# A hybrid encoder layer with 32 experts: from the eleventh unit on, the down projection goes ahead of the next up projection

## The reference, cut to what matters

```python
def hier_moe(x, w_group, b_group, w_router, b_router, w_e1, w_e3, w_e2):
    ...
    for gi in range(N_GROUPS):
        h = jax.nn.silu(jnp.einsum('md,edf->mef', xt, w_e1[gi])) * jnp.einsum('md,edf->mef', xt, w_e3[gi])
        out = out + jnp.einsum('mef,efd->md', h * combine[:, gi, :, None], w_e2[gi])
    return out.reshape(n, t, d)
```

## Time and profile before

| what | value |
|---|---|
| median of 3 runs | 898.16 us |
| the three runs | 896.39, 898.16, 898.18 us |
| the profiled execution's own time | 896.4 us |
| its span in the profile | 894.6 us |
| PE busy | 765.0 us, 86% |
| DVE, ACT, POOL busy | 363.6, 228.2, 156.5 us |
| DMA, mean over the span | 196 GB/s |
| HBM read | 164.43 MB |

### The profile page before, as it was taken

The page is one execution under the profiler, slowest core; times in us unless marked ns, Lnnn a source line. Parts: engine busy times, 40 slices in busy tenths (PEclk is TensorE's granted clock), DMA queues, the critical chain, the costliest instruction groups (busy, mean ns, idle before and its releaser), DMA issues.

```text
span 894.6 us, 11943 instructions
## 1 busy us (share of the span) xinstructions
PE 765.0 (86%) x4700; PEld 554.5 (62%) x4700; DVE 363.6 (41%) x632; ACT 228.2 (26%) x444; POOL 156.5 (17%) x157
## 2 busy tenths in 40 slices
PE   6999999999799999999999999953999996476600
PEld 6999985774466999999999954531333332122100
DVE  4899927997676310110111022465111111010168
ACT  5214231736576522222222100110111111010100
POOL 4000001000313243335333300012011111000100
PEclk9999999999898999999999999975999999688955
DMA  8323225021100732222222078484999999999872
GB/s 327 139 75 97 77 71 188 13 66 38 47 1 13 277 113 83 84 74 83 81 83 95 13 287 370 153 348 165 390 418 417 419 421 420 420 420 421 307 262 82
DMA packets 38467, 175.73 MB, mean 196 GB/s; under 512 B 7064, under 2 KB 7624, under 8 KB 25992
## 3 DMA queue, kind: packets, MB, share of 16 engines
q1 hardware_dynamic: 33496, 163.66, 47.7%
q0 software_dynamic: 4912, 11.28, 3.4%
HBM read 164.43 MB, written 16.78 MB: 203 GB/s over the span
## 4 chain that ended last, share of the span: by engine, by line
PE 73%; DMA 9%; DVE 8%; SPq 7%; issue 2%; ACT 1%; POOLq 0%; ACTq 0%
PE PS L673 38%; PE PS L975 7%; PE PS L865 7%; DMA expert<-in_w_e 7%; PE PS L656 5%; SPq L495 4%; PE PS L997 3%; PE PS L783 2%; SPq L498 2%; PE PS L749 2%; PE PS L763 2%; PE PS L731 2%; DVE x_tiles L1699 1%; PE PS L826 1%; PE PS L929 1%
## 5 line engine op out<-in xcount | busy, mean ns | idle before, releaser
L673 PE MATMUL PS<-x_hi,w_hi 128*128 128x288 f32 (+2 forms) x656 | 142.5, 299 | 9.4 <-DVE x_lo L1310 8.5
L673 PE MATMUL PS<-x_lo,w_hi 128*128 128x288 f32 (+2 forms) x656 | 141.9, 298 | 0.0
L673 PE MATMUL PS<-x_hi,w_lo 128*128 128x288 f32 (+2 forms) x656 | 141.6, 298 | 0.0
L975 PE MATMUL PS<-expert,moe_tmp 128*64 128x512 f32 (+2 forms) x576 | 112.5, 630 | 31.3 <-DMA expert<-in_w_e 30.0
L673 PEld LDWEIGHTS PS<-x_hi,w_hi 128*128 128x128 f32 x656 | 106.7, 191 | 9.7 <-POOL w_lo L455 8.5
L1060 ACT ACTIVATE w_hi<-raw_ring 128x1024 fp32r<-128x1024 f32 (+1 forms) x57 | 57.1, 1002 | 214.4 <-PE PS L673 209.9
L673 PEld LDWEIGHTS PS<-x_lo,w_hi 128*128 128x128 f32 x656 | 106.6, 191 | 0.0
L673 PEld LDWEIGHTS PS<-x_hi,w_lo 128*128 128x128 f32 x656 | 106.5, 191 | 0.0
L975 PEld LDWEIGHTS PS<-expert,moe_tmp 128*64 128x64 f32 (+2 forms) x576 | 36.1, 134 | 97.4 <-issue 95.5
L455 POOL TENSOR_TENSOR w_lo<-raw_ring,w_hi 128x1024 fp32r<-128x1024 f32 (+1 forms) x33 | 70.2, 2127 | 136.3 <-ACT w_hi L1060 136.3
L1327 DVE SCALAR_TENSOR_TENSOR conv_z<-attn_tmp,wdw,conv_z 128x576 f32<-128x576 f32 x120 | 90.6, 813 | 0.3
(11 more groups left out here) (286 smaller groups left out, 1021.1 us busy)
## 6 DMA issues: line engine op xcount, KB each, us to landing
expert<-in_w_e SPq DMA_DIRECT2D x96, 1024.0 KB, 26.2
raw_ring<-in_w_gate_t SPq DMA_DIRECT2D x24, 512.0 KB, 3.3
raw_ring<-in_w_glu_t SPq DMA_DIRECT2D x8, 512.0 KB, 4.8
raw_ring<-in_w_como_t SPq DMA_DIRECT2D x8, 512.0 KB, 3.5
heads<-in_w_out SPq DMA_DIRECT2D x1, 4096.0 KB, 14.0
x_rows<-x_tiles SPq DMA_DIRECT2D x8, 512.0 KB, 5.1
expert_out<-expert_rows SPq DMA_DIRECT2D x8, 512.0 KB, 6.5
x_raw<-in_xT SPq DMA_DIRECT2D x4, 576.0 KB, 6.0
```

The source lines that it names most:

```text
L673: mm = pe.matmul(half(name, s, 128, cols[s]), w[:, n % 2, at + 128 * k:at + 128 * k + 128], x[:, k, t0[s]:t0[s] + cols[s]], start=(k == 0 ...
L975: mm = pe.matmul(PS[r0:r0 + nr, 2, :].rearrange("p (s f) -> p s f", s=2), xgT[:, k, r0:r0 + nr], w13[s % NB][:, :, k, :], start=(k == 0), ...
```

## The change

A constant `UNPIPED = 10` is added. For u below 10 the order stays. For u from 10 to 14 `result_step(u - 1)` stands at the head of the loop's body, ahead of the up projection of u (`hidden_step(u)`, on ScalarE `silu_step(u)`), in place of behind `rows_step(u + 1)`. This is done on the three engines TensorE, ScalarE and VectorE. No instruction is added or removed, and nothing changes in the queues of SP and GpSimd.

```diff
+UNPIPED = 10
@@ TensorE; the same on VectorE @@
             for u in range(1, NS):
+                if u >= UNPIPED:
+                    result_step(u - 1)
                 hidden_step(u)
                 if u + 1 < NS:
                     rows_step(u + 1)
-                result_step(u - 1)
+                if u < UNPIPED:
+                    result_step(u - 1)
                 hidden_turn_step(u)
             result_step(NS - 1)
```

## The result

The changed kernel takes 902.15 us, median of 6 runs (901.21 to 903.67), against 897.62 us for the kernel before in 6 runs. The ratio is 1.0056, with a 95% interval of 1.0044 to 1.0068: it is slower by 5.0 us by the ratio and by 4.5 us by the medians. Forecast were 902.6 us and a span of 899.6. Of the 5.9 us between the two spans, 0.6 us are there before the experts begin: TensorE's first turned rows start at 618.35 in place of 617.71.

The account below looks back on a forecast made before the run. Expert weights coming through one DMA queue were taken to bound the last third. Plus 9.0 us at TensorE, minus 4.0 at the last scatter, gave plus 5.0, span 899.6; predicted 902.6 us, between 901.4 and 903.2, range 899.4 to 906.8.

Parts of the forecast that it names:

- The new wait: Before unit 13's down projection: about 6.2 us waiting for expert 29's down weights, with unit 14's up projection queued behind.
- The landing: Expert 29's down weights land at 833.2 instead of 832.5, as unit 12's scatter now goes in front.
- The clock: After the pause, unit 13's down projection runs at the low clock level, 5.85 us instead of 3.62: 2.2 us.
- Rival B: TensorE keeps the high clock level through the wait, or the wait is shorter: plus 2.8, 899.2 to 901; chance 0.10.
- Turn and product of unit 14 uncovered: Near the end, TensorE waits 1.0 us for VectorE's product, then 1.07 us for turn and evacuation.
- TensorE's last step: The last down projection ends at 851.9 instead of 842.92, 9.0 us later.
- What is given back: The last scatter, now without other loads, takes 4.0 us instead of 7.97: minus 4.0.
- Rival A: The last scatter does not get quicker: plus 9.0 us, 905.4 to 907.2; chance 0.16.
- Units 10 to 12 at no cost: Moved down projections there cost 0, at most 1 us; unit 11's up projection may start 1 to 2.5 us later.
- A sign of being wrong that came up: Loads of unit 11's slots issued more than 3 us off 778.7 or 805.4 would show the prediction wrong.
- Rival C: No measurable change, expert 29's down weights land earlier, each microsecond before 833.2 gaining one: 897.5 to 899; chance 0.09.
- D: Faster: unit 12's down projection fills the earlier wait, weights land before 828: minus 1.5, 896.7; chance 0.05.

Follow-up runs that it names:

- experiment 1: Only the down projection of unit 13 goes ahead of the up projection of unit 14, units 10 to 13 in old order; ratio 1.0031 to the kernel before.
- experiment 2: Down projections moved ahead in units 10 to 13 only, unit 14 in the old order; ratio 0.9985 to the kernel before.
- experiment 5: The kernel before with three 1 MB expert weight transfers left out, outputs wrong, only times read; ratio 0.9993 to the kernel before.
- experiment 6: The changed kernel with three 1 MB expert weight transfers left out, outputs wrong, only times read; ratio 0.9938 to the kernel before.
- experiment 3: Only the down projection of unit 12 goes ahead of the up projection of unit 13; ratio 0.9989 to the kernel before.
- experiment 4: The changed kernel with 14 idle matmuls ahead of the wait of unit 13's down projection, keeping the clock up; ratio 1.0027 to the kernel before.
- experiment 8: The kernel before with unit 13's step alone moved, x rows loaded after the last scatter and norm vectors earlier; ratio 0.9951 to the kernel before.
- experiment 9: The changed kernel measured again, unaltered; ratio 1.0053 to the kernel before.
- experiment 10: The changed kernel with x rows loaded behind the scattered results and norm vectors earlier; ratio 1.0054 to the kernel before.
- experiment 7: The kernel before with x rows loaded behind the scattered results and norm vectors earlier, away from the last scatter; ratio 0.9956 to the kernel before.

## Why the prediction was right, point by point

- **The new wait.** Forecast: down 13 ready at 827.0 and held until 833.2 by the down weights of expert 29. Measured: ready at 827.6, when ScalarE had evacuated its turn, and start at 834.69. Experiments 1 and 2 put the wait on unit 14's step, experiments 5 and 6 on the landing: with it gone, the loss is gone.
- **The landing 1.4 us later than forecast** (834.55, forecast 833.2). The whole stream stands 0.8 us later in this execution (down 11 starts at 800.14 in place of 799.32), and 0.6 us of that is there before the experts begin. Counted from the start of down 11, the weights of expert 29 land after 33.2 us in the kernel before and 33.3 in experiment 1, where the scatter of unit 12 is issued only 2 to 4 us ahead of them; and after 34.4 to 34.6 us in the changed kernel and in experiments 3, 4, 8, 9 and 10, where it is issued over 10 us ahead. Experiment 3 moves no scatter but this one. So this scatter, moved in front of the landing, costs 1.2 us, where I had taken 0.7. That fits its half megabyte at 420 GB/s, but that its bytes are the reason is not tested apart.
- **The clock.** Forecast 2.2 us for down 13; against the 3.64 us of experiment 4 it was 2.1 us in the first profile of the changed kernel (5.72), 1.9 in experiment 10 (5.52) and 1.3 in experiment 9 (4.92). The forecast lies above all of them. Rival B, that TensorE keeps the high level, falls. In experiment 1 the pause was 4.0 us, and the clock fell only when down 13 had begun (0.77 in 834 to 835, 0.50 in 835 to 836); the step took 5.34 us all the same.
- **Turn and product of unit 14 uncovered.** Forecast 1.0 and 1.07 us; in the rows after, 0.94 us of waiting before the turn and 0.91 from the turn to down 14.
- **TensorE's last step** came 10.0 us later, 9.0 were forecast. Down 13 started 1.5 us later than forecast; down 13 itself gave 0.3 back (5.66 us to the start of up 14, 6.0 forecast) and the steps behind it the rest. The 839.2 of the prediction is 0.15 too high by its own terms (833.2 plus 5.85), and the fall of the clock at 848 to 849 came 5.4 us after TensorE's end, not 5.7 (a mean of 0.65 puts it at about 848.3); neither changes the result.
- **What is given back.** Forecast 4.0 us, measured 4.4 in the profile (3.53 in place of 7.97). Rival A, that the scatter stays at 8 us, is ruled out, and experiment 7 shows why. Behind it the loads of the first tile took 4.70 us in place of 4.33, a term that I had put at nothing.
- **Units 10 to 12 at no cost.** Right in the sum (experiment 2), wrong in one place: I had no wait there, but down 9, now ahead of up 10, waited 6.79 us for its weights until 745.57 and took 5.93 us at a mean clock of 0.60. This cost nothing, because 11.25 us of waiting before up 11 were still left. Up 11 started at 775.25, 2.1 us later, within the 1 to 2.5 forecast; but that the moved scatter and gather are the reason is not shown, since experiment 1, with the old order up to unit 13, has nearly the same time from the first turned rows to up 11 (156.8 us, changed 156.9, before 155.5).
- **A sign of being wrong that came up.** I had written that I am wrong if the loads of unit 11's slots are issued more than 3 us off 778.7. They were issued 3.2 us later:

```profile
781.88 15.31 SPq L497 DMA_DIRECT2D expert<-in_w_e  x8
```

Up 11, which releases them, began 2.1 us later and ran slower (9.86 us in place of 8.76). The landing did not follow: the DMA engines stayed busy (share 1.01 from 781.88 to 800), and down 11 started only 0.8 us later. The backlog that the prediction counted on held, and the limit of 3 us was drawn too narrow.

- **Rival C and D.** The rule that an earlier landing gives the time back held, and experiment 6 went past it: with the landing before 827 the new order is 5.6 us faster, where I had allowed 1.5. The mis-sized terms are the scatter, which took 3.44 us where I had 6 beside fewer loads, and TensorE's end, which came 0.5 us earlier than before (counted from down 11) where I had 0.6 later.
- **Where the number was lucky.** The forecast of 902.6 is 0.45 us from the measured median of 902.15, well inside the spread of the six runs (901.21 to 903.67), so that nearness is luck. The mechanism and the two large terms are shown by the experiments, but the errors cancel in part: TensorE lost 1.0 us more than forecast and the loads of the first tile 0.4, the scatter gave 0.4 more back, and the median of the kernel before was 897.62 us in six runs where I had started from 898.16.

## What to carry to other kernels

Where a stream of weights bounds a stretch, the place of a step is good or bad by the transfer that it waits for: put the step whose data are already there ahead of the one whose data come last, and keep the longest ready step for the longest wait. Follow the chain from the last landing that the remaining work needs; moving work out from behind it pays only until the next landing in the queue decides, here after 0.4 us in the profile (experiment 3, 43.2 in place of 43.6 us), which the times don't tell from nothing. And look at what else is on the DMA engines when a short transfer ends the chain: loads that are only needed later can wait until it is through.

## What the runs showed of the hardware

- The last indirect scatter of 128 rows took 3.1 to 3.7 us where little or nothing else was on the DMA engines (a share of 0.24 to 0.29, scatter included; the changed kernel and experiments 1, 4, 6, 7, 8, 9 and 10) and 7.8 to 8.2 us beside the loads for the last norm (0.88 to 0.94; the kernel before and experiments 2, 3 and 5). The scatters of the kernel before, all in company, took 7.8 to 9.7 us. I had only a gather (4.0 us) to take this from.
- The same half of an up projection (32 rows, second half of unit 13) took 4.93 to 6.21 us after waits of 5.95 to 7.37 us, in the profiles of the kernel before and of experiments 1, 3, 5, 7 and 8. So a step behind a pause has a spread of over 1 us, more than most terms of this sum.
